# The first tap of the recurrent branch's convolution, on GpSimd in place of ScalarE

## The reference, cut to what matters

```python
def directional_conv(x, w, b, reverse):      # width 4, depthwise
    kw = w.shape[0]; s = x.shape[1]
    if reverse:
        xp = jnp.pad(x, ((0, 0), (0, kw - 1), (0, 0)))
        y = sum(w[k] * xp[:, k:k + s] for k in range(kw))
    else:
        xp = jnp.pad(x, ((0, 0), (kw - 1, 0), (0, 0)))
        y = sum(w[k] * xp[:, kw - 1 - k:kw - 1 - k + s] for k in range(kw))
    return y + b

xf = directional_conv(xr, rnn_conv_w[i, 0], rnn_conv_b[i, 0], False)
xb = directional_conv(xr, rnn_conv_w[i, 1], rnn_conv_b[i, 1], True)
hr = rg_lru(xf, ...) + rg_lru(xb, ..., reverse=True)
```

## Time and profile before

| what | value |
|---|---|
| median of 3 runs | 949.04 us (949.01 to 949.27) |
| the profiled execution | 949.1 us, of which the span of its instructions is 947.3 us |
| PE | 927.0 us busy, 98% of the span |
| DVE | 729.6 us, 77% |
| ACT | 577.1 us, 61% |
| POOL | 1.4 us, 9 instructions |
| granted TensorE clock | 0.997 of full |

### The profile page before, as it was taken

One profiled execution on the slowest core, in us unless ns is written; L12 is line 12 of the kernel. 1 busy time (PEld: TensorE's weight loads), 2 busy tenths in 40 slices (PEclk: granted clock), 3 DMA queues, 4 the chain that ended last, 5 costly groups with the idle time before them and its releaser, 6 DMA issues.

```text
span 947.3 us, 12574 instructions
## 1 busy us (share of the span) xinstructions
PE 927.0 (98%) x5100; PEld 800.1 (84%) x5100; DVE 729.6 (77%) x981; ACT 577.1 (61%) x730; POOL 1.4 (0%) x9
## 2 busy tenths in 40 slices
PE   5999999999999999999999999999999999999996
PEld 3898988988888888888889889888888888888885
DVE  5888898787867867767868698888878676866755
ACT  4578899764356644555345889987435564545540
POOL 0000000000000000000000000000000000000000
PEclk9999999999999999999999999999999999999998
DMA  9546444584485555566443644456656656555521
GB/s 333 153 163 200 136 156 157 185 305 164 156 266 182 199 198 178 192 203 204 160 161 119 211 159 155 134 180 197 256 179 217 226 187 205 186 180 198 201 89 45
DMA packets 118457, 174.62 MB, mean 184 GB/s; under 512 B 3968, under 2 KB 78976, under 8 KB 117888
## 3 DMA queue, kind: packets, MB, share of 16 engines
q1 hardware_dynamic: 118256, 173.79, 55.0%
q10 hardware_dynamic: 144, 0.03, 0.0%
HBM read 172.76 MB, written 1.05 MB: 183 GB/s over the span
## 4 chain that ended last, share of the span: by engine, by line
PE 88%; DVE 7%; ACT 4%; DMA 0%; issue 0%; DVEq 0%; ACTq 0%
PE ring L548 13%; PE ring L550 13%; PE ring L549 13%; PE ring L601 9%; PE ring L597 9%; PE misc L548 5%; PE misc L549 5%; PE misc L550 5%; PE ring L600 5%; PE ring L598 5%; PE misc L778 2%; DVE sb_w_lo L1253 2%; PE ring L721 1%; PE misc L837 1%; ACT sb_w_hi L933 1%; DVE sb_tmp L1485 1%
## 5 line engine op out<-in xcount | busy, mean ns | idle before, releaser
L1253 DVE TENSOR_TENSOR sb_w_lo<-sb_raw,sb_w_hi 128x2048 fp32r<-128x2048 f32 x138 | 294.8, 2148 | 65.8 <-ACT sb_w_hi L933 65.8
L933 ACT CAST sb_w_hi<-sb_raw 128x2048 fp32r<-128x2048 f32 x138 | 246.3, 1796 | 19.6 <-DMA sb_raw<-in_w_out_dram 4.3
L601 PE MATMUL ring<-sb_x_both,sb_w_hi 128*128 128x512 f32 x272 | 107.6, 396 | 0.0
L597 PE MATMUL ring<-sb_x_both,sb_w_hi 128*128 128x512 f32 x272 | 107.5, 395 | 0.0
L548 PE MATMUL ring<-sb_w_hi,sb_x_both 128*128 128x512 f32 x272 | 107.1, 394 | 0.0
L549 PE MATMUL ring<-sb_w_lo,sb_x_both 128*128 128x512 f32 x272 | 106.0, 390 | 0.0
L550 PE MATMUL ring<-sb_w_hi,sb_x_both 128*128 128x512 f32 x272 | 106.0, 390 | 0.0
L600 PE MATMUL ring<-sb_x_both,sb_w_lo 128*128 128x256 f32 x272 | 75.7, 278 | 0.0
L598 PE MATMUL ring<-sb_x_both,sb_w_lo 128*128 128x256 f32 x272 | 75.4, 277 | 0.0
L548 PE MATMUL ring<-sb_x_both,sb_w_hi 128*128 128x256 f32 x256 | 72.6, 284 | 0.0
L550 PE MATMUL ring<-sb_x_both,sb_w_lo 128*128 128x256 f32 x256 | 72.4, 283 | 0.0
(11 more groups left out here) (229 smaller groups left out, 2111.8 us busy)
## 6 DMA issues: line engine op xcount, KB each, us to landing
sb_raw<-in_w_in_dram SPq DMA_DIRECT2D x40, 1024.0 KB, 5.3
sb_raw<-in_w_up_dram SPq DMA_DIRECT2D x34, 1024.0 KB, 5.2
sb_raw<-in_w_down_dram SPq DMA_DIRECT2D x18, 1024.0 KB, 5.0
sb_raw<-in_w_proj_attn_dram SPq DMA_DIRECT2D x8, 1024.0 KB, 5.2
sb_raw<-in_w_proj_rnn_dram SPq DMA_DIRECT2D x8, 1024.0 KB, 5.1
sb_hb<-in_w_up_dram SPq DMA_DIRECT2D x8, 1024.0 KB, 5.3
sb_raw<-in_w_out_dram SPq DMA_DIRECT2D x6, 1024.0 KB, 6.2
sb_raw<-in_w_ple_gate_dram SPq DMA_DIRECT2D x6, 1024.0 KB, 5.4
```

Of the source, the lines that this page charges most:

```text
L597: nc.tensor.matmul(bank_of(*key), hi[:, cols], x_both[:, k], start=k == 0, stop=False)
L601: last = nc.tensor.matmul(bank_of(*key), hi[:, cols], x_both[:, k + 1], start=False, stop=k + 2 == KT)
L933: nc.scalar.copy(hi_at[home][:, at], raw_at[home][:, at]).then_inc(s_hi_part, 1)
L1253: nc.vector.tensor_tensor(lo_at[home][:, 0:size], raw_at[home][:, 0:size], hi_at[home][:, 0:size].bitcast(F32), ALU.subtract).then_inc(s_s ...
```

## The change

The two instructions of `conv_base` move from ACT's list to POOL's. On POOL they stand in a loop of their own over the layers and the eight blocks, with the same three waits: parameters loaded, the xr bank read out, and the slot of xc free. Each of the two instructions now raises `s_conv_base` (before, only the second did), so the counts double. ACT's list loses its eight calls per layer. Nothing else moves.

```diff
-    param_step=16, param_exp=1, conv_base=8, conv_step=48, rin_hi=8, rin_ready=8,
+    param_step=16, param_exp=1, conv_base=16, conv_step=48, rin_hi=8, rin_ready=8,
...
+            def conv_base(l, i):
+
+                direction, b = divmod(i, RNN_BLOCKS)
+                if i == 0:
+                    pool.wait_ge(s_small, 32 * l + 32)
+                xr = (l, f"xr{b // 2}", b % 2)
+                pool.wait_ge(s_emptied[RING[xr][0]], read_out(*xr))
+                pool.wait_ge(s_gated, value("gated", l, max(0, i - 1)))
+                for j in range(2):
+                    ft = 2 * b + j
+                    nc.gpsimd.tensor_scalar(xc[:, i % 2, j, :], xT[:, ft, :], rnnp[:, direction, ft, 0:1],
+                                            rnnp[:, direction, ft, 4:5], ALU.mult, ALU.add).then_inc(s_conv_base, 1)
+
+            for l in range(DEPTH):
+                for i in range(2 * RNN_BLOCKS):
+                    conv_base(l, i)
...
-            def conv_base(l, i):
-
-                direction, b = divmod(i, RNN_BLOCKS)
-                if i == 0:
-                    act.wait_ge(s_small, 32 * l + 32)
-                xr = (l, f"xr{b // 2}", b % 2)
-                act.wait_ge(s_emptied[RING[xr][0]], read_out(*xr))
-                act.wait_ge(s_gated, value("gated", l, max(0, i - 1)))
-                for j in range(2):
-                    ft = 2 * b + j
-                    last = nc.scalar.activation(xc[:, i % 2, j, :], xT[:, ft, :], ACT.Identity,
-                                                bias=rnnp[:, direction, ft, 4:5], scale=rnnp[:, direction, ft, 0:1])
-                last.then_inc(s_conv_base, 1)
...
-                conv_base(l, 0)
...
-                conv_base(l, 1)
...
-                conv_base(l, 2)
...
-                    if i + 2 < 2 * RNN_BLOCKS:
-                        conv_base(l, i + 2)
...
-                dve.wait_ge(s_conv_base, value("conv_base", l, i + 1))
+                dve.wait_ge(s_conv_base, value("conv_base", l, 2 * i + 2))
```

## The result

| | before | after |
|---|---|---|
| median | 949.06 us (948.87 to 949.85, 8 runs) | 951.62 us (951.48 to 952.72, 8 runs) |
| span of the profiled execution | 947.3 us | 949.3 us |
| time outside the span | 1.8 us | 2.18 us |

The change makes the kernel 0.26% slower: the ratio is 1.0026, with a 95% interval from 1.0015 to 1.0037. The two profiled executions differ by 2.4 us (949.1 and 951.48): 2.0 inside the span and 0.4 outside it. The time outside is each run's time less its span; it is the same for every run of a kernel to within 0.1 us. Some runs of most kernels are 0.8 to 1.2 us late by the time PE has come to 21 us, so a median can lie some tenths above the bulk of its runs.

A forecast was written before the change was run, and what follows sets the result against it. PE was taken to bound the kernel, with its work plus its waits. Two layers of +1.05 us on DVE at block 4, and 0 won elsewhere, added 2.1 to 949.04 for 951.1 us; the range was 948.7 to 952.6.

The forecast's parts named there:

- turn-taking at block 4: POOL's pair and DVE's two-input instructions before block 4's taps exclude each other: +1.05 us a layer, 951.1 us, chance 0.58.
- 950.9: Upper bound of "the same" for the whole kernel's time; a measurement tells about 0.2%, 1.9 us, from no change.
- ACT's relief: 0.99 us off ACT's chain at block 5 closes the `sb_ga` wait but is spent at the transposes; costed at 0.
- the slack of 0: At PE's transposes of `turn_probs`, round 1, at 128.74: slack between 0 and 0.20 us, taken as 0.
- The sign named for this: In the changed kernel, PE's wait on `sb_ga`, 0.4 us a layer before, would be gone or smaller.
- POOL's price: Each moved 128x256 instruction on POOL: 0.41 us, bounds 0.32 and 0.60; a pair with 0.23 start 1.05 us.
- The reason that I took from the rows: DVE takes 350 ns for 256 columns with one SBUF tensor, 479 with two: reading sets its pace, no spare path.
- two ways that I left open: At block 4, POOL's pair enters DVE's list either ahead of the split or ahead of the taps; same sum.
- The sum: Per layer +1.05 us on DVE at block 4 and 0 elsewhere: 2.1 us on 949.04, giving 951.1.
- The other blocks are covered: Pairs of all blocks but 4 cost 0, hidden by pauses or slack; block 6's rest of about 0.6 us included.
- Hidden: Rival: POOL reads beside DVE in block 4's 2.77 us window, leaving only 0 to 0.2 us won a layer: 948.9; chance 0.27.
- POOL is slow: Rival: POOL's instructions take some 0.7 us or more each; at 1.2 us, with turns, 954.3 us; chance 0.13.

The follow-up runs named there:

- the one with the maximum on DVE: Changed kernel plus one DVE instruction between L1503 and the split of stage 2, a maximum reading one SBUF tensor: 952.14 us, ratio 1.0031 to the kernel before.
- taking back block 6: Changed kernel with the pairs of blocks 4 and 6 back on ACT, the other six of a layer on POOL: 949.31 us, ratio 0.9999 to the kernel before.
- writing-only kernel: Changed kernel with POOL setting xc to zero by memset in place of the first tap: 949.74 us, ratio 1.0007 to the kernel before.
- block 4 in a place of its own: Changed kernel with block 4's xc in the part of `hb` that block 7 fills later: 949.91 us, ratio 1.0011 to the kernel before.

## Why the prediction was right

The forecast was 951.1 us, slower by turn-taking at block 4; 951.62 was measured, within its range. The mechanism was the one forecast. On which side of 950.9 the time would fall was close to a toss-up, though: by the prediction's own chances the same (0.51) stood slightly before slower (0.47), and the mixers' loss of 0.92 + 0.93 = 1.85 us alone would have given 950.9, right on that bound. What took the time clearly past that bound are two terms that the sum did not have. Step by step:

- **ACT's relief is worth nothing.** Right. With block 4 on ACT, and with no first tap at all, the wait on `sb_ga` closes and PE waits 0.4 us at the transposes instead; neither kernel is faster than before. This also bears out the slack of 0 that I took there: the two gain 0.02 to 0.06 us in a mixer. The sign named for this, a wait on `sb_ga` gone or smaller, hardly showed in the changed kernel (0.7 us after 0.8), since the exponentials ahead of that copy come 0.8 us later there.
- **POOL's price.** 0.41 us was too low. The median is 0.557, within the bounds of 0.32 and 0.60; a pair on its own takes 1.09. The Trainium skill's price (an estimate of 0.38 for one instruction, from the page "GPSIMD Engine Reference", section 3.1) is too low here as well.
- **Turns, not side by side.** Right, shown by POOL's 3.50 us at block 4, by the kernel in which POOL reads nothing and by the one with the maximum on DVE. The reason that I took from the rows does not hold, though: at 1024 columns DVE takes 1.22 us with two SBUF inputs (the split at 94.41 in the kernel before, below) and 1.21 with one (the maximum), so the number of inputs does not show in its pace. The 350 and 479 ns that I compared belong to different operations. As far as that reason goes, it was luck that turns came true. The Trainium skill's rule (page "SBUF — State Buffer", "SBUF: two separate sides" and "Who interferes with whom") agrees in what conflicts: two SBUF inputs on DVE against a POOL operation that reads SBUF; the memsets were not held and the one-input maximum did not hold. Of the two ways that I left open it was the second: the pair was not done between DVE's L1503 and the split, but ahead of the taps.

```profile
94.41 1.22 DVE L1253 TENSOR_TENSOR sb_w_lo<-sb_raw,sb_w_hi 128x1024 fp32r<-128x1024 f32 x1
```

- **The sum.** 1.05 us a layer was mis-sized in its parts, with errors that nearly cancel, which is luck. POOL's start of 0.23 was hidden behind DVE's split, and the first instruction needed only 0.27 us after it (to 99.22), the second 0.53 more: DVE waited 0.84, and its taps came 0.92 late. PE lost 0.94 and 0.93 against what its own pace allowed, and 0.92 and 0.93 against the kernel before. So 1.9 us in place of 2.1.
- **The other blocks are covered.** Right. Doubling blocks 2, 3 and 5 and taking back block 6 changed nothing. Blocks 0 and 1 in layer 0 stood behind DVE's splits too (pairs of 1.86 and 2.44 us), and PE lost nothing there. Block 6's delay was 1.0 us, not 0.6: the pause of 0.47 before its split was ACT's, and it closed.
- **What was missing.** 0.4 us outside the span, with ACT's shorter list, and 0.3 us after DVE's last instruction, in the last store (946.0 to the span's end at 949.3, where it was 944.3 to 947.3). With the two mixers that makes 1.85 + 0.3 + 0.4, less 0.15 for an earlier start, the 2.4 us between the two profiled executions. The 0.3 us do not grow with POOL's work: the stretch takes 3.3 to 3.4 us in the five kernels with 41 POOL instructions and 3.0 in all others, those with 45 and 53 (the pairs done twice) among them. Why is open.
- **The rivals.** "Hidden" is ruled out by 0.84 us of waiting, and holds for the writing-only kernel. "POOL is slow" was wrong in size: 0.557 is below its 0.7.

## What to carry to other kernels

Before work is moved to POOL beside a busy DVE, look at what DVE runs between the moment the work is released and the moment its result is wanted: instructions with two SBUF inputs, back to back, shut POOL's reading out to the end (2.96 us here, for an instruction of 0.557), however much time the window seems to hold. What that costs is decided by whether DVE's next step has slack; here 4 of 32 instructions made the loss in the mixer, and releasing them one stage earlier took it away. An engine that waits most of the time is not a place to win from: when its one visible wait closes, read which gate the bound engine meets next.

## What was not expected of the hardware

- Both can be held, and POOL can be passed over. An instruction of POOL that was released during a two-input instruction of DVE stayed for 2.96 us instead of 0.557, and the next DVE instruction went ahead of it. The other way round DVE gives way. In the changed kernel L1503 began at 147.83, when 0.23 us of a POOL instruction (to 148.06) were left, and took 0.765 us where the median is 0.694:

```profile
146.96 1.09 POOL L553 TENSOR_SCALAR sb_tmp<-sb_xT,sb_rnnp 128x256 f32<-128x256 f32 x2 [11.52 <-DVE sb_hb L1499]
```

```profile
147.83 0.77 DVE L1503 SCALAR_TENSOR_TENSOR sb_scan_in<-sb_tmp,sb_scan_in 128x512 f32<-128x512 f32 x1 [1.04 <-ACT sb_tmp L1019]
```

With 0.41 us left it took 0.94 (block 4 in a place of its own, at 77.88), so DVE loses what is left of POOL's instruction less some 0.16 us. The Trainium skill's rule (page "SBUF — State Buffer", section "SBUF: two separate sides") that whoever starts first keeps the other out for the whole instruction fits this but for these last 0.16 us. A waiting POOL instruction, though, stays out across the boundary between two DVE instructions.
- After DVE's last two-input instruction a held POOL instruction needs 0.43 us at block 6 (134.47 to 134.90), and only 0.27 at block 4. The split of block 4 takes 2.32 and 2.31 us where it took 2.29; whether POOL got in for a moment ahead of it is not shown.
- With 24 to 32 ACT instructions fewer, the time outside the span goes from 1.8 us either nowhere (706) or to 1.95 (702) and 2.1 to 2.2 (698), whatever POOL does.
